# Attention's steps on TensorE in one group per round, with VectorE's scaling as a step of its own

## What is computed

```python
yA = forgetting_attention(heads(qA), heads(kA), heads(vA), fA, forget_bias[l])   # 8 heads, causal, a bias of its own
yB = dsa_attention(rope(qB), rope(kB), vB, rope(qI), rope(kI), wI)               # 8 heads, the 128 best keys
r  = retention(rope(qC), rope(kC), vC)                                           # 8 heads, no softmax
yD = sliding_window_gqa(rope(qD), rope(kD), vD, attn_sinks[l])                   # 8 heads, window of 128
branch = jnp.einsum('bsnc,ncd->bsnd', jnp.stack([yA, yB, yC, yD], 2), w_branch[l])
x = x + jnp.sum(jax.nn.sigmoid(gates) * branch, axis=2) @ w_out[l]
```

## Time and profile before

| | us |
|---|---|
| median of 3 runs | 3756.16 |
| lowest and highest | 3754.97, 3762.64 |
| the profiled execution, its own time | 3761.97 |
| span of its instructions | 3760.4 |
| TensorE matmul busy | 3535.6 (94%) |
| TensorE weight load busy | 2781.5 (74%) |
| VectorE busy | 1709.0 (45%) |
| ScalarE busy | 1465.5 (39%) |
| GpSimd busy | 1418.1 (38%) |
| mean granted clock of TensorE | 0.966 of full |

### The profile page before, as it was taken

How to read it: one execution, slowest core, us unless ns; L and a number is a source line. 1 busy time by engine, 2 the same in 40 slices (tenths; PEclk the granted TensorE clock), 3 DMA queues, 4 the chain that set the end, 5 groups by cost and what they waited for, 6 DMA issues and landing times.

```text
span 3760.4 us, 45163 instructions
## 1 busy us (share of the span) xinstructions
PE 3535.6 (94%) x17424; PEld 2781.5 (74%) x17424; DVE 1709.0 (45%) x3129; ACT 1465.5 (39%) x2478; POOL 1418.1 (38%) x651
## 2 busy tenths in 40 slices
PE   6899989898799999999999999999989999989998
PEld 4788889785578876767766778887866766678886
DVE  7886553557420116845542233134755552334133
ACT  3223453554432233344443334343335443334342
POOL 3554433321244444324332344444323332344443
PEclk9999999999899998999999999998989999999999
DMA  7574354221122322211122222323212222223332
GB/s 292 192 249 146 129 158 160 69 90 45 45 89 90 101 88 66 73 51 62 68 79 71 87 79 89 102 92 96 79 45 62 62 68 85 79 79 90 101 94 80
DMA packets 109974, 364.90 MB, mean 97 GB/s; under 512 B 12608, under 2 KB 13504, under 8 KB 109504
## 3 DMA queue, kind: packets, MB, share of 16 engines
q1 hardware_dynamic: 107280, 356.33, 29.4%
q10 hardware_dynamic: 2480, 5.68, 0.4%
HBM read 359.86 MB, written 2.10 MB: 96 GB/s over the span
## 4 chain that ended last, share of the span: by engine, by line
PE 76%; DVE 13%; ACT 5%; issue 3%; DMA 1%; POOL 1%; SPq 0%; DVEq 0%; POOLq 0%; ACTq 0%
PE ps L1306 24%; PE ps L1308 22%; PE ps L1307 22%; PE ps L1550 2%; ACT b L1634 1%; PE ps L1571 1%; DVE b L2169 1%; DVE b L2462 1%; PE ps L1532 1%; DVE b L2461 1%; DVE b L2205 1%; DVE b L2150 1%; POOL b L2533 1%; PE ps L1605 1%; PE ps L1528 1%
## 5 line engine op out<-in xcount | busy, mean ns | idle before, releaser
L2533 POOL TENSOR_TENSOR b<-b,b 128x1024 fp32r<-128x1024 f32 (+2 forms) x579 | 1324.2, 2287 | 2050.5 <-ACT b L1634 2045.6
L1306 PE MATMUL ps<-b,b 128*128 128x512 f32 (+3 forms) x4848 | 1868.3, 385 | 93.4 <-POOL b L2533 27.0
L1307 PE MATMUL ps<-b,b 128*128 128x512 f32 (+3 forms) x4848 | 1807.7, 373 | 0.0
L1308 PE MATMUL ps<-b,b 128*128 128x512 f32 (+3 forms) x4848 | 1807.1, 373 | 0.0
L1306 PEld LDWEIGHTS ps<-b,b 128*128 128x128 f32 x4848 | 936.7, 193 | 362.4 <-issue 153.2
L1308 PEld LDWEIGHTS ps<-b,b 128*128 128x128 f32 x4848 | 936.4, 193 | 160.5
L1307 PEld LDWEIGHTS ps<-b,b 128*128 128x128 f32 x4848 | 938.5, 194 | 144.8 <-issue 4.8
L1634 ACT ACTIVATE b<-b 128x1024 fp32r<-128x1024 f32 (+2 forms) x622 | 607.2, 978 | 270.3 <-PE ps L1308 236.5
L2073 DVE SCALAR_TENSOR_TENSOR b<-ps,b,b 128x511 f32<-128x511 f32 x88 | 66.0, 750 | 371.0 <-ACT b L1685 371.0
L2169 DVE CUSTOM_DVE_ANT_0 b<-b,b,b 128x1024 bf16<-128x1024 f32 x112 | 212.1, 1894 | 16.7 <-DMA b<-in_ada 4.9
L1695 ACT ACTIVATE b<-b 128x512 fp32r<-128x512 f32 (+1 forms) x110 | 64.9, 590 | 389.3 <-DVE b L2082 286.9
(11 more groups left out here) (235 smaller groups left out, 2376.7 us busy)
## 6 DMA issues: line engine op xcount, KB each, us to landing
b<-in_w SPq DMA_DIRECT2D x458, 512.0 KB, 3.5
b<-in_ada SPq DMA_DIRECT2D x88, 512.0 KB, 5.0
b<-in_w SPq DMA_DIRECT2D x80, 384.0 KB, 3.1
b<-in_w SPq DMA_DIRECT2D x80, 320.0 KB, 2.8
b<-in_const SPq DMA_DIRECT2D x24, 256.0 KB, 3.9
b<-in_x SPq DMA_DIRECT2D x1, 2048.0 KB, 16.8
out<-b SPq DMA_DIRECT2D x8, 256.0 KB, 2.5
b<-in_c SPq DMA_DIRECT2D x2, 512.0 KB, 10.0
```

The source lines that it names most:

```text
L1306: pe.matmul(out, a[0], b[0], start=first, stop=False)
L1307: pe.matmul(out, a[0], b[1], start=False, stop=False)
L1308: return pe.matmul(out, a[1], b[0], start=False, stop=last)
L2533: then(pool.tensor_tensor(wlo[j % NS][:, 0:nk * w], raw[j % NR][:, 0:nk * w], whi[j % NS][:, 0:nk * w].bitcast(F32), ALU.subtract), "lop", j)
```

## The change

1. In `heads` the three steps of a round stand together, as one list that `weave` puts in as a whole, with no triple between them. In the retention `c2` and `c1` of a round do the same.
2. VectorE's reciprocals and scalings leave `s2` and become a step `sp2`, which is put in half a round ahead of the group that holds the round's `s2`. TensorE's and ScalarE's parts of `s2` stay in the group.
3. The rates fall, since a round is now two items in place of three (or one in place of two): 0.8 to 0.57 in A, 0.6 to 0.435 in B and D, 0.55 to 0.35 in C. A round thus comes about as often as before in A, B and D: every 5.5 triples in A, every 7.2 in B and D.
4. In stage A the four rotary tiles of qb no longer stand ahead of the eight tiles of gt; each stands behind two of them. `plan()` lists the weights in the same new order, in chunks of the same size.

```diff
@@ plan
-                cols("gt", w2, l, GT, 1024)
...
-        cols("qb", w2, l, QB, 512)
+        for m in range(4):
+            cols("gt", w2, l, GT + 256 * m, 256)
+            cols("qb", w2, l, QB + 128 * m, 128)
@@ Fore
-    def rope(self, name, count, key, **kw):
-        for m in range(count):
+    def rope(self, name, count, key, at=0, **kw):
+        for m in range(at, at + count):
@@ weave
-    out, due, back = [], 0.0, list(back)
+    out, due, back = [], 0.0, [b if isinstance(b, list) else [b] for b in back]
...
-                out.append(back.pop(0))
-    return out + back
+                out += back.pop(0)
+    return out + [s for b in back for s in b]
@@ schedule, heads
-                if k >= 3:
-                    out.append(do("s3", a=kind, l=l, w=k - 3))
                 if 0 <= k - 2 < len(PAIRS):
-                    out.append(do("s2", a=kind, l=l, w=k - 2))
-                if k < len(PAIRS):
-                    out.append(do("s1", a=kind, l=l, w=k))
+                    out.append(do("sp2", a=kind, l=l, w=k - 2))
+                out.append([do(s, a=kind, l=l, w=w) for s, w in (("s3", k - 3), ("s2", k - 2), ("s1", k))
+                            if 0 <= w < len(PAIRS)])
@@ schedule, stage A
-        F.rope("qb", 4, "qb", ver=H, l=l)
-        for m in range(8):
-            t = F.fm("gt", m, "gt", H, L, o=0, l=l)
-            F.step("evac", t=t)
-        S += weave(F, heads("A"), 0.8) + [do("takey", l=l, o=0, t=t) for t in range(4)]
+        for m in range(12):
+            if m % 3 == 2:
+                F.rope("qb", 1, "qb", at=m // 3, ver=H, l=l)
+            else:
+                t = F.fm("gt", m - m // 3, "gt", H, L, o=0, l=l)
+                F.step("evac", t=t)
+        S += weave(F, heads("A"), 0.57) + [do("takey", l=l, o=0, t=t) for t in range(4)]
@@ schedule, stages B, D (both) and C
-        S += weave(F, heads("B"), 0.6) + [do("takey", l=l, o=1, t=t) for t in range(4)]
+        S += weave(F, heads("B"), 0.435) + [do("takey", l=l, o=1, t=t) for t in range(4)]
...
-            if k >= 2:
-                B.append(do("c2", l=l, w=k - 2))
-            if k < len(PAIRS):
-                B.append(do("c1", l=l, w=k))
+            B.append([do(c, l=l, w=w) for c, w in (("c2", k - 2), ("c1", k)) if 0 <= w < len(PAIRS)])
...
-        S += weave(F, B, 0.55) + [do("takey", l=l, o=3, t=t) for t in range(4)]
+        S += weave(F, B, 0.35) + [do("takey", l=l, o=3, t=t) for t in range(4)]
@@ dve_program (number() marks the event pr in the new step in the same way)
-            elif k == "s2":
+            elif k == "sp2":
```

More of the change, by code:

```diff
@@ L515, in schedule @@
         branch(F, 1, 1)
-        S += weave(F, heads("D"), 0.6) + [do("takey", l=l, o=2, t=t) for t in range(4)]
+        S += weave(F, heads("D"), 0.435) + [do("takey", l=l, o=2, t=t) for t in range(4)]
         F = fore()
@@ L881, in number @@
                 mark("ex", *u)
+        elif k == "sp2":
+            for p in range(2):
+                mark("pr", s["a"], s["l"], 2 * s["w"] + p)
         elif k == "s2":
@@ L885, in number @@
                 u = (s["a"], s["l"], 2 * s["w"] + p)
-                mark("pr", *u)
                 mark("tp", *u)
```

## The result

The changed kernel takes **3793.74 us** (median of 4 runs, 3790.37 to 3796.25), the kernel before beside it 3759.4 (3754.97 to 3763.63). The ratio is 1.0091, with a 95% interval of 1.0077 to 1.0105: slower by 0.9%, some 34 us. Forecast were 3721 and a range of 3692 to 3745.

A forecast was written before the change was run, and what follows sets the result against it. TensorE, busy 94% of the span, was taken as the bound, so only its idle time, half clock and changes between matmul kinds could be won. The terms summed to −35.3 us, from 3756.2 to 3721 us, range 3692 to 3745.

The forecast's parts named there:

- The scalings ahead: In front of the transposes: scalings put half a round ahead end all of TensorE's waits for them, −28.5 us.
- The clock: Half-clock stretches behind the waits for the scaling, 17.06 us in layer 0, 17.07 in layer 1: half comes back, −17.1.
- The rotary bank is late next: Transposes in A, B and D wait for the last rotary tile's bank, free only after part 3: 7.4 per layer, +14.8.
- Longer scalings: VectorE's scalings held up by GpSimd's subtraction: some 0.1 us for each of 48, +4 us, an estimate.
- vc's banks: Where vc tiles hold four banks, two groups' logits per layer wait for ScalarE's copies: 2.2 per layer, +4.4 us.
- The start of C: First products with values come later, so their waits of 5.3 us and 3.4 of half-clock loss go: −8.7.
- The start of A: First logits stand one triple later, filling 0.69 of each wait of 3.0 us: −1.4; the half clock behind stays.
- The joints: Closed gaps between TensorE's matmul kinds: 0 in A, B and D (bounds −37 to +17), −2.8 us in C.
- the first (the wait only changes its name): Rival: TensorE waits as long for rotary parts; 24 bank waits of 1.6 us cost 38.4, giving 3744.5; chance 0.14.
- The second (groups halve the clock): Rival: groups of small matmuls run at half clock in A, B and D; half of 114 gives 3818 us; chance 0.07.
- the third: Rival: neither rotary bank nor vc is late (−23.2), each closed gap saves 0.10 (−17): 3681 us; chance 0.17.
- L2436 still ending waits of 2 to 3 us: Sign in the changed profile: the scaling still ends TensorE's long waits, meant to show that the wait only changes its name.

## Why the prediction was wrong

By its own steps, in its order, for both layers; the forecast first, then the profile of the changed kernel:

- **The scalings ahead** (−28.5): 28.5 us of waits became 7.4, so −21.1. The mechanism was right, but it isn't the step's doing alone: A's waits of all kinds, 10.3 us per layer before and 5.5 in layer 0 now, are 1.5 by the interleaving alone and 6.0 in the change without it.
- **The clock** (−17.1, and 3.4 in C's start): the long waits for the scaling in A went with their stretches, but one or two stretches per layer stand there behind what came in their place, and the new waits of B and D brought more. In sum the loss rose by 20.3 us where 20.5 were to be won, a miss of 41 us that follows from the next one. The term was also 2 us too large: part of each stretch lies in the wait itself, and TensorE was busy for 15.14 and 14.98 us of the two layers' 17.06 and 17.07.
- **The rotary bank is late next** (+14.8): it was 60.4 us, and 3.8 more in front of a chunk's matmul: a miss of 49 us, the largest. Here the prediction failed. It had the place, the order in VectorE's queue and the distances right, and it took the two scalings between the parts at "0.9 to 1.2" us, from clean rows. At the eight groups of B and D that waited long they took 2.2 to 4.0, from the end of the part ahead to the start of the next. The run without the long subtraction gives the size of the two halves: 30 us are the collision (some 4 of them `takey`'s, which no step of the forecast had); of the other 30, the term covers 14.8. Layer 0 of that run shows waits of 1.3, 1.7 and 1.6 where 0.3, 0.9 and 1.6 were forecast (groups at 6, 5 and 4 triples in B), and 2.2 and 1.9 at the first groups of B and D, where a distance of seven triples was said to leave nothing. There ScalarE's copy is late: in D of the changed kernel it starts at 1849.72, right behind the exponentials of the group just ahead.
- **Longer scalings** (+4): the step that failed in its reasoning. It named the collision, cited a row of 2.43 us for it, and then spread it as a mean of 0.1 over 48 scalings. A collision isn't a mean. Before, 12 of 192 scalings were above 1.2 us; now 22 are, and since rotary copy, subtraction and scaling step recur in fixed order, it struck ten of the 16 rotary tiles of a layer's stages (once the sum of two columns in place of a scaling), at the one place where TensorE waits for what stands behind. Over both layers, the tiles so struck are the 20 at which TensorE waited for the bank. "The change neither adds nor removes such a pair" was true of the instructions and false of their timing.
- **vc's banks** (+4.4): 1.6 us, four waits as forecast.
- **The start of C** (−8.7): shown right by the retention alone; the 5.3 us and the half clock went.
- **The start of A** (−1.4): 6.0 became 4.6, exact.
- **The joints** (−2.8, between −37 and +17): −25.5. The step "the same four changes as before, I take 0" was wrong for A, B and D, as the timeline of a group in A shows:

```profile
1637.65 0.39 PE L1309 MATMUL ps<-b,b 128*128 128x512 f32 x1
1637.97 1.09 PE L1572 MATMUL ps<-b,b 128*64 128x128 f32 x16
1638.99 0.44 PE L1551 MATMUL ps<-b,b 128*128 128x128 f32 x2
1639.36 0.92 PE L1529 MATMUL ps<-b,b 64*128 64x384 f32 x4
...
1640.38 0.50 PE L1307 MATMUL ps<-b,b 128*128 128x512 f32 x1
1640.72 0.39 PE L1308 MATMUL ps<-b,b 128*128 128x512 f32 x1
```

The group pays 0.32 once to get in (1637.65 to 1637.97) and 0.34 once for the first full matmul behind it (1640.38 to 1640.72), in place of 0.23 each; inside it a step begins 0.20 behind the last small matmul of the step ahead, where small matmuls of one step stand 0.11 to 0.16 apart. Before, `s3` and `s1` paid both prices, and `s2` only the one behind it (0.23 on the way in, 0.31 on the way out):

```profile
1639.30 0.40 PE L1308 MATMUL ps<-b,b 128*128 128x512 f32 x1
1639.53 0.82 PE L1550 MATMUL ps<-b,b 128*128 128x128 f32 x6
1640.11 0.47 PE L1306 MATMUL ps<-b,b 128*128 128x512 f32 x1
1640.42 0.40 PE L1307 MATMUL ps<-b,b 128*128 128x512 f32 x1
```

By these rows a closed gap saves some 0.02 us between `s3` and `s2` and 0.14 between `s2` and `s1` (an estimate). Counting changes of mode, as the forecast did, gave nothing; the joints with the triples cost more than those between the steps. Grouping against no grouping gives 0.06 per joint there and up to 0.3 in the retention. These give some 18 of the 25.5; the rest, in size about what B won, is not accounted for.

The rivals: the first (the wait only changes its name) is what happened, under a price of 24 waits of 1.6; it was given 0.14 and an end at 3744.5, since it had no clock and no collision in it. The second (groups halve the clock) didn't happen: no half-clock stretch in the stages stands without a wait at or just ahead of it, and with the scaling a round ahead, D keeps a clock of 1.00 with every group in place. Of the third, the joints came true while its other half turned over; its −23.2 also held the 4.0 for longer scalings, since the bank and vc alone make 19.2. The sign that the prediction named, "L2436 still ending waits of 2 to 3 us", would have cleared rival 1 wrongly; it was L2151 that ended them.

Put right with what the runs show, the sum is −21.1 (scalings) + 60.4 + 3.8 (bank) + 20.3 (clock, all) + 1.6 (vc) − 5.3 (C) − 1.4 (A) − 3.1 (`rn1`) − 25.5 (joints) = +29.7, beside 28.5 in the spans.

## What to carry to other kernels

When a step is moved in an in-order queue, list what now runs on the neighbouring engine at its new time, not only what stands around it in its own queue; a conflict that was rare by chance can become one per period when both sides recur in the same order. If something holds a buffer for which the bound engine waits, nothing may stand between the operations that free it: moving VectorE's step by half a round, ahead of the rotary tile, turned +34 us into −51. And price each lost microsecond of such a wait with the clock: here 34 us of new idle time brought 20 more.

## What the runs showed of the hardware

- What GpSimd's subtraction holds up on VectorE goes by where the inputs lie. Of the instructions that began inside it in the attention stages, rotary parts (one input in PSUM) lasted as ever (0.69, 4 of 4 in the changed kernel and 38 of 38 in the kernel before), and so did the masked maxima (44 of 44, 0.28 to 0.69 by their size); the scalings lasted 1.6 to 2.5, to just past the subtraction's end (22 of 22). Even a `tensor_tensor` of two single columns ended with the subtraction (6 of 6; 1.75 and 2.33 us, twice each, in place of 0.15), while a reciprocal or `tensor_scalar` on one column wasn't held (0.16 and 0.15). The second line here is the sum of two columns at D's first group, which alone made TensorE wait 1.6 us longer (3.46 in place of 1.88 in the run with the short subtraction):

```profile
1850.32 2.08 DVE L2151 TENSOR_TENSOR b<-ps,b 32x512 f32<-32x512 f32 x3 [1.42 <-ACT b L1732]
1852.42 1.75 DVE L2434 TENSOR_TENSOR b<-b 128x1 f32<-128x1 f32 x1
1854.21 0.16 DVE L2435 RECIPROCAL b<-b 128x1 f32<-128x1 f32 x1
```

- The clock followed waits of 1.4 us too. In the kernel before, stalls of 1.3 to 1.6 us left it whole; in the changed one it was halved for 3.41 us behind a wait of 1.39 (at 1961.54), and behind one of 1.80 with 0.79 just after it in layer 1, though not behind the same pair in layer 0.
